# x read channel-major from the host's layout with 1/rms spread by two GpSimd transfers, y turned by DMA transposes, and latents first, in a hybrid attention layer

## The chip, the cores and the metric

The kernel runs on one core of one Trainium2 chip. The metric is device time in microseconds (us) of one execution, the median of several. TensorE (PE in the rows) has a weight-load side of its own (PEld); VectorE is DVE, ScalarE ACT, GpSimd POOL. SP only issues transfers here; SPq and ACTq are the streams of transfers that SP and ScalarE issue. The transfers of all of them run on the same 16 DMA engines of the core.

## The reference, cut to what matters

x is 2048 tokens by 1024 channels, float32. One layer:

```python
h = x + W_out( concat[ GQA(xn) * silu(g_A), MLA(xn) * silu(g_B) ] ), xn = RMSNorm(x)

y = xf * lax.rsqrt(jnp.mean(xf * xf, axis=-1, keepdims=True) + EPS) * g      # rms_norm
proj = xn @ w_in          # 2464 columns: q, k, v, gate of A; query latent, kv latent, rotary key, gate of B
c_q = rms_norm(b_cq), c_kv = rms_norm(b_ckv)                                 # the latents, 384 and 256 wide
qb = c_q @ w_uq ; kvb = c_kv @ w_ukv                                         # queries, keys and values of B
# per-head rms_norm and 2-D rotary on q and k, softmax attention over all 2048 tokens, 8 heads of A, 4 of B
y = concat[y_a * silu(a_g), y_b * silu(b_g)] ; h = x + y @ w_out
```

## The kernel before, in words

The work is in three phases that follow one another; phase 2 (attention) is not touched. Every large product is taken in three float16 matmuls: a float32 operand is split into a high part (its float16 rounding) and a low part (the rest), and high*high, high*low and low*high are summed. ScalarE makes high parts, VectorE low parts.

**Phase 1** (`phase1`) goes over 16 tiles of 128 tokens. TensorE contracts over partitions, so its left operand `xT` must have channels on partitions, and x arrives with tokens on them. For tile t: ScalarE squares and sums x (`x_hi`, L372), takes the root, VectorE the reciprocal (`x_rstd`, L494), ScalarE writes x * 1/rms as float16 (`xh`, L379), VectorE the rest (`x_lo`, `xl`, L502); TensorE turns both by 16 products with the identity (`transpose_x`, L659), and VectorE copies them out of PSUM (`xt_evac`, L508). The turn of tile t+1 lies inside tile t, between the products `ukv1` and `bg`. TensorE's order inside a tile is `cq, ckv, aq, akv`, the turn of the latents (`transpose_latents`, L671), `ag, uq, ukv0, ukv1`, the turn of x for the next tile, `bg` (all products L639); the last two tiles run a slightly other list (`LATE`), in which tile 14 has no `bg` of its own. Its results go through three PSUM banks (`ring`), which ScalarE empties (`evac`, L385). Head norms and rotary are a long chain on VectorE (L559 to L609), which begins when `ukv1` has been read out and squared (L461), and ends in the next tile; then `z_hi` and `z_lo` (L392, L514) split the finished rows, and two DMA transposes on SP's queue (`turn_z`, L307, L309) turn them, 13 blocks of 128x128 each. On both engines the steps of a tile stand in the order: x of the next tile and z of the one before, then the latents. In the first tile the weights are split as they arrive (`split_hi` L409, `split_lo` L522; pieces 0 to 7 are `cq, ckv, uq, ukv, aq, akv, ag, bg`), through raw buffers that SP refills when a piece has been split. A transfer on SP's queue waits in order: what stands behind a waiting one isn't issued.

**Phase 3** (`phase3`) again goes over 16 tiles: load the gate pre-activations G and attention outputs YA, YB (`load_yg`, L1220 to L1222), silu on ScalarE (L1257), gate on VectorE (L1295, L1296), split into `yh` (ScalarE, L1272) and `yl` (VectorE, L1323), turn both on TensorE (`turn`, L1342; that of tile t+1 lies between the two output halves of tile t), copy the turned tiles out of PSUM on ScalarE (`yT`, L1282), 48 matmuls of 512 columns (L1356), add the residual on VectorE (L1306), store (L1235). SP issues all loads and stores; its order in tile t is loads of t+2, then the wait for the residual of t, its store, and the load of x for t+2. On VectorE the gate of t+1 stands before the residual of t-1.

Of the kernel before, what the change touches and what calls it, by code (L numbers as in the profile page):

```python
# [24 lines left out]
P = 128  # L25
# [54 lines left out]
def phase1(nc, early, x, w_in, w_uq, w_ukv, g_in, g_cq, g_ckv, g_heads, trig, eye, QA, QBd, KBd, VA, VB, G):  # L80
    with ExitStack() as ctx:
# [17 lines left out]
        xin = sb("xin", [P, 2, D])  # L99
# [3 lines left out]
        xh = sb("xh", [P, D], F16)  # L103
        xl = sb("xl", [P, D], F16)
# [23 lines left out]
        xtp = [ps(f"xtp{i}", [P, KT, P], F16) for i in range(2)]  # L128
# [4 lines left out]
        s_x = [sem("x_loaded0"), sem("x_loaded1")]  # L133
# [7 lines left out]
        s_ax = sem("act_x_chain")  # L141
        s_dx = sem("dve_x")
        s_xtp = sem("xT_in_psum")
        s_xt = sem("xT_in_sbuf")
# [101 lines left out]
        def _(sp):  # L246
            sp.dma_start(xin[:, 0, :], xt[0]).then_inc(s_x[0], 16)
# [4 lines left out]
            for n in range(len(pieces)):  # L252
# [14 lines left out]
            def tile(i, h, first, last):  # L267
# [6 lines left out]
                if not last:  # L274

                    sp.wait_ge(s_dx, t * 2 + 2)
                    sp.dma_start(xin[:, h, :], xt[t + 2]).then_inc(s_x[h], 16)
# [75 lines left out]

        @block.gpsimd
        def _(pool):
            pool.memset(va[:, :, 2 * DA:2 * DA + 1], 1.0).then_inc(s_ones, 1)
# [8 lines left out]

        @block.scalar
        def _(act):
            def x_hi(t, h):

                st = stat[:, h, :]  # L370
                act.wait_ge(s_x[h], x_count(t, h))
                act.activation(junk[:, 0:D], xin[:, h, :], ACT.Square, accum_out=st[:, 0:1]).then_inc(s_ax, 1)  # L372
                act.wait_ge(s_ax, t * 3 + 1)
                act.activation(st[:, 1:2], st[:, 0:1], ACT.Sqrt, bias=eps[:, :], scale=1.0 / D).then_inc(s_ax, 1)
                act.wait_ge(s_dx, t * 2 + 1)
                if not zero(t):

                    act.wait_ge(s_xtp, t * 2)
                act.activation(xh[:, :], xin[:, h, :], ACT.Copy, scale=st[:, 2:3]).then_inc(s_ax, 1)  # L379
# [31 lines left out]
            def tile(i, h, first, last):  # L411
# [3 lines left out]
                if not (last and h == 1):  # L415
                    x_hi(t + 1, 1 - h)
# [990 lines left out]
```

## Time and profile before

| | |
|---|---|
| median of 3 runs | 1676.17 us (1674.85 to 1676.73) |
| the profiled execution's own time | 1674.67 us |
| its span, from first to last instruction | 1672.5 us |
| phase 1, until the first instruction of phase 2 | about 0 to 532 us |
| phase 2 | about 532 to 1463 us |
| phase 3 | about 1463 to 1672.5 us |
| TensorE busy over the span | 1566.9 us, 94% |
| VectorE, ScalarE, GpSimd | 71%, 65%, 34% |
| the 16 DMA engines | 38.2% |

Shares over the whole span mix three stages with different limits, so they say little about this change, which touches the first and the last. What counts is which wait ends last in each of these two, and that is read from the timeline of each engine and from the chain of waits. The profiled execution lies 1.5 us under the median.

### The profile page before, as it was taken

To read this page: it belongs to the slowest core of one execution; us is meant where nothing else is said; L and a number is where in the kernel's file an instruction comes from. 1 tells how busy PE (TensorE), PEld (TensorE's weight loads), DVE (VectorE), ACT (ScalarE), POOL (GpSimd) and SP (SyncE) were. 2 spreads that over 40 slices of the span, in tenths; PEclk is the share of its full clock that TensorE was granted. 3 is DMA by queue.
4 is the path that set the end of the run, shared out by engine and by line. 5 is a ranking of instruction groups with operands and counts; after the bars stand their busy time and mean duration, and the time that the engine had idled before them with its cause. 6 is when DMAs were issued, how large, how long until landed. Compare 5 with 4: busy or idle time off the path is not lost. (4 is left out here: it accounts for less than half of the span.)

```text
span 1672.5 us, 38256 instructions
## 1 busy us (share of the span) xinstructions
PE 1566.9 (94%) x13808; PEld 914.9 (55%) x13808; DVE 1181.3 (71%) x1664; ACT 1083.8 (65%) x1410; POOL 565.4 (34%) x478
## 2 busy tenths in 40 slices
PE   5899999999993799999999999999999999869998
PEld 2456555565551355665566556656665665534444
DVE  6665464654644889988998899889888988443322
ACT  8444444444431588888888888888888888643322
POOL 0100000000000356666666566656666665600000
PEclk9999999999996899999999999999999999979999
DMA  8343343353246422432243224322432243045563
GB/s 299 94 113 92 92 127 88 100 127 92 79 98 144 150 64 64 92 79 62 59 95 79 62 59 95 79 62 59 95 78 63 59 95 75 15 151 184 168 193 109
DMA packets 296351, 166.77 MB, mean 100 GB/s; under 512 B 118256, under 2 KB 279536, under 8 KB 296304
## 3 DMA queue, kind: packets, MB, share of 16 engines
q1 hardware_dynamic: 295824, 165.97, 38.2%
q8 instruction: 27, 0.44, 0.1%
q10 hardware_dynamic: 480, 0.20, 0.0%
q14 instruction: 20, 0.16, 0.0%
HBM read 109.85 MB, written 40.92 MB: 90 GB/s over the span
## 5 line engine op out<-in xcount | busy, mean ns | idle before, releaser
L940 POOL TENSOR_TENSOR p_pl<-p_p,p_ph 128x512 f16<-128x512 f32 x384 | 502.0, 1313 | 789.7 <-ACT p_ph L976 729.8
L991 DVE TENSOR_REDUCE p_part<-p_mx 128x2 f32<-128x1024 f32 x384 | 468.3, 1220 | 86.2 <-PE p_mx L1067 68.3
L967 ACT ACTIVATE p_p<-p_st 128x1024 f32<-128x1024 f32 x384 | 391.3, 1019 | 125.9 <-PE p_st L1099 68.1
L639 PE MATMUL p_ring<-p_w_hi,p_xT 128*128 128x512 f16 (+3 forms) x1536 | 389.2, 339 | 13.5 <-DVE p_w_lo L522 10.3
L976 ACT ACTIVATE p_ph<-p_p 128x1024 f16<-128x1024 f32 x336 | 355.3, 1057 | 18.3
L1019 DVE TENSOR_TENSOR p_pl<-p_p,p_ph 128x512 f16<-128x512 f32 x384 | 325.8, 849 | 10.3 <-ACT p_ph L976 9.4
L639 PE MATMUL p_ring<-p_w_lo,p_xT 128*128 128x512 f16 (+3 forms) x768 | 260.2, 339 | 0.0
L639 PEld LDWEIGHTS p_ring<-p_w_hi,p_xT 128*128 128x128 f16 x1536 | 151.1, 98 | 136.0 <-issue 12.9
L1131 PE MATMUL p_acc<-p_vas,p_ph 128*128 128x129 f16 x2048 | 207.9, 221 | 0.0
L1132 PE MATMUL p_acc<-p_vas,p_pl 128*128 128x65 f16 x2048 | 201.0, 193 | 0.0
L1131 PEld LDWEIGHTS p_acc<-p_vas,p_ph 128*128 128x128 f16 x2048 | 180.6, 97 | 36.4 <-issue 14.3
L1098 PE MATMUL p_st<-early 128*128 128x512 f16 x512 | 194.7, 380 | 0.0
L1099 PE MATMUL p_st<-early 128*128 128x512 f16 x512 | 194.6, 380 | 0.0
L1132 PEld LDWEIGHTS p_acc<-p_vas,p_pl 128*128 128x128 f16 x2048 | 181.4, 98 | 13.5
L1135 PE MATMUL p_acc<-p_vbs,p_ph 128*128 128x129 f16 x1024 | 185.9, 221 | 0.0
L1137 PE MATMUL p_acc<-p_vbs,p_pl 128*128 128x129 f16 x1024 | 184.6, 222 | 0.0
L1136 PE MATMUL p_acc<-p_vbs,p_ph 128*128 128x128 f16 x1024 | 184.2, 219 | 0.0
L1356 PE MATMUL p_po<-p_w_hi,p_yT 128*128 128x512 f16 x512 | 158.8, 383 | 8.7 <-ACT p_yT L1282 4.3
L1067 PE MATMUL p_mx<-early 64*128 64x512 f16 x512 | 104.4, 404 | 45.7 <-DVE p_kb L1041 24.5
L1135 PEld LDWEIGHTS p_acc<-p_vbs,p_ph 128*128 128x128 f16 x1024 | 100.9, 99 | 50.4 <-issue 39.9
L639 PEld LDWEIGHTS p_ring<-p_w_lo,p_xT 128*128 128x128 f16 x768 | 75.5, 98 | 53.6 <-issue 0.5
L508 DVE COPY p_xT<-p_xtp 128x1024 f16<-128x1024 f16 x32 | 20.7, 686 | 117.8 <-PE p_xtp L659 117.8
(130 smaller groups left out, 2027.4 us busy)
## 6 DMA issues: line engine op xcount, KB each, us to landing
p_vbs<-scratch_vb SPq DMA_DIRECT2D x16, 1028.0 KB, 6.1
p_xin<-in_x SPq DMA_DIRECT2D x16, 512.0 KB, 3.8
scratch_g<-p_g SPq DMA_DIRECT2D x16, 512.0 KB, 2.6
p_kb<-scratch_kb SPq DMA_DIRECT2D x32, 256.0 KB, 5.3
p_gt<-scratch_g SPq DMA_DIRECT2D x16, 512.0 KB, 4.7
p_xr<-in_x SPq DMA_DIRECT2D x16, 512.0 KB, 4.1
out<-p_res SPq DMA_DIRECT2D x16, 512.0 KB, 3.0
early<-in_w_in SPq DMA_DIRECT2D x6, 1024.0 KB, 7.0
```

Source lines behind the costliest of these rows:

```text
L639: last = pe.matmul(ring_t[:, 0:w], a, b, start=(k == 0 and m == 0), stop=(k == len(steps) - 1 and m == len(terms) - 1))
L940: pool.tensor_tensor(pl[:, s % NP, 1, :], p32[:, s % N32, QB:], ph[:, s % NP, 1, :], ALU.subtract).then_inc(s_lop, 1)
L967: act.activation(p32[:, s % N32, :], st[:, s % 2, :, :].rearrange("p a b -> p (a b)"), ACT.Exp, scale=scale).then_inc(s_exp, 1)
L976: act.activation(ph[:, s % NP, :, :].rearrange("p a b -> p (a b)"), p32[:, s % N32, :], ACT.Copy).then_inc(s_hi, 1)
L991: dve.tensor_reduce(part[:, e // MPAIRS % 3, 2 * c:2 * c + 2], mx[:, :, :], AX, ALU.max).then_inc(s_red, 1)
L1019: dve.tensor_tensor(pl[:, s % NP, 0, :], p32[:, s % N32, 0:QB], ph[:, s % NP, 0, :], ALU.subtract).then_inc(s_lo, 1)
L1098: pe.matmul(out, ka_hl[g][:, keys], qa_hh[g][:, :], start=True, stop=False)
L1099: end = pe.matmul(out, ka_up[g][:, keys], qa_ml[g][:, :], start=False, stop=True)
L1131: pe.matmul(a, hi, vas[:, t, g, :], start=new, stop=False, skip_group_check=True)
L1132: last = pe.matmul(a[:, DA:], lo, vas[:, t, g, DA:], start=False, stop=end, skip_group_check=True)
L1135: pe.matmul(a, hi, vbs[:, t, DVB:], start=new, stop=False, skip_group_check=True)
L1137: last = pe.matmul(a, lo, vbs[:, t, DVB:], start=False, stop=end, skip_group_check=True)
```

## The change

In phase 1, x is read a second time, channel-major (`x_cols`, laid out by the host: for each tile a 128-partition block of 8 x 128 tokens). The token-major copy (`xin`, now one buffer) serves only for the sum of squares. The 128 values 1/rms of a tile stand one per partition; two transfers issued by GpSimd write them to DRAM (`RS`) and read them back as a row copied to all partitions (`rsb`). VectorE multiplies `xcol` by it in place (`x_scale`), ScalarE writes the high part straight into `xT`, VectorE the low part. TensorE's turn of x, the PSUM tiles `xtp` and `xt_evac` are gone. The statistics of a tile are taken two tiles ahead. In a tile, both engines now do the latents before z and x. In the first tile, the statistics of tiles 0 and 1 and the whole of x for tile 0 stand between `split(0)` and `split(1)`.

In phase 3, `yh` and `yl` get two buffers each and are turned by two DMA transposes on SP's queue (8 blocks each); TensorE's turn, the PSUM tiles `tp` and ScalarE's copies are gone. From tile 2 on, ScalarE issues `load_yg`, after the silu of the next tile; SP keeps the transposes, the store and the x load.

```diff
@@ phase 1, SP
+                if n == 0:
+                    sp.dma_start(xcol[:, :, :], x_cols[0]).then_inc(s_xc, 16)
                 if n == 1:
-                    sp.dma_start(xin[:, 1, :], xt[1]).then_inc(s_x[1], 16)
+                    load_x(1)               # waits s_ax >= 2
+                if n == 3:
+                    load_x(2)               # waits s_ax >= 4
+                if n == 4:
+                    sp.wait_ge(s_xt, 1)
+                    sp.dma_start(xcol[:, :, :], x_cols[1]).then_inc(s_xc, 16)
@@ phase 1, GpSimd
+        def spread_rstd(eng, t):
+            eng.wait_ge(s_dx, t + 1)
+            eng.dma_start(RS[t], stat[:, t % 2, 2:3]).then_inc(s_rs, 16)
+            eng.wait_ge(s_rs, t * 16 + 16)
+            if t > 1:
+                eng.wait_ge(s_xs, t - 1)
+            eng.dma_start(rsb[:, t % 2, :], RS[t].partition_broadcast(P)).then_inc(s_rsb[t % 2], 16)
@@ phase 1, VectorE
+            def x_scale(t, h):
+                dve.wait_ge(s_xc, t * 16 + 16)
+                dve.wait_ge(s_rsb[h], (t - h) * 8 + 16)
+                dve.tensor_tensor(xcol[:, :, :], xcol[:, :, :], rsb[:, h, :].unsqueeze(1).to_broadcast([P, KT, P]),
+                                  ALU.mult).then_inc(s_xs, 1)
             def x_lo(t, h):
+                dve.wait_ge(s_xh, t + 1)
+                dve.tensor_tensor(xT[:, h, 1], xcol[:, :, :], xT[:, h, 0], ALU.subtract).then_inc(s_xt, 1)
@@ phase 1, VectorE, before the loop
             x_rstd(0, 0)
-            x_lo(0, 0)
-            xt_evac(0, 0)
-            dve.wait_ge(s_const, 64)
-            for n in range(5):
+            dve.wait_ge(s_const, 64)
+            split_lo(0)
+            x_rstd(1, 1)
+            x_scale(0, 0)
+            x_lo(0, 0)
+            for n in range(1, 5):
                 split_lo(n)
@@ phase 1, TensorE
-                if not (last and h == 1):
-                    transpose_x(t + 1, 1 - h)
@@ phase 3, SP
+            def turn(t, h, free):
+                sp.wait_ge(s_yh, t + 1)
+                if free:
+                    sp.wait_ge(s_po, t * 2 - 2)
+                sp.dma_start_transpose(yT[:, h, 0], yh[:, h, :]).then_inc(s_yt[h], 16)
+                sp.wait_ge(s_yl, t + 1)
+                sp.dma_start_transpose(yT[:, h, 1], yl[:, h, :]).then_inc(s_ytl[h], 16)
             def tile(t, h, i, first, last):
-                if not last:
-                    sp.wait_ge(s_yg, t * 2 + 2)
-                    load_yg(t + 2, h)
+                if not (last and h == 1):
+                    turn(t + 1, 1 - h, not (first and h == 0))
                 sp.wait_ge(s_res, t * 2 + 2)
                 sp.dma_start(ot[t], res[:, h, :]).then_inc(s_out[h], 16)
@@ phase 3, ScalarE, tile t
-                for s in range(2):
-                    act.wait_ge(s_tp, t * 2 + s + 1)
-                    if not first:
-                        act.wait_ge(s_po, t * 2 - 2)
-                    act.activation(yT[:, h, s], tp[s][:, :, :], ACT.Copy).then_inc(s_yt, 1)
+                if not last:
+                    load_yg(act, t + 2, h)
@@ phase 3, TensorE, tile t
-                    if c == 0 and not (last and h == 1):
-                        turn(t + 1, False)
```

The first place is ScalarE in tile 1 of phase 1, from the gate's read-out (`p1_g`) on. Before:

```order
L372 ACTIVATE p1_junk,p1_stat<-p1_xin 128x1024
L374 ACTIVATE p1_stat<-p1_stat,p1_eps 128x1
L379 ACTIVATE p1_xh<-p1_xin,p1_stat 128x1024
L392 ACTIVATE p1_zh<-p1_R 128x640
L393 ACTIVATE p1_zh<-p1_R 128x8x96
L385 ACTIVATE p1_cq32<-p1_ring0 128x384
L385 ACTIVATE p1_ckv32<-p1_ring1 128x288
L426 ACTIVATE p1_junk,p1_lstat<-p1_cq32 128x384
```

and with the change:

```order
L403 ACTIVATE p1_junk,p1_stat<-p1_xin 128x1024
L407 ACTIVATE p1_stat<-p1_stat,p1_eps 128x1
L421 ACTIVATE p1_cq32<-p1_ring0 128x384
L421 ACTIVATE p1_ckv32<-p1_ring1 128x288
L460 ACTIVATE p1_junk,p1_lstat<-p1_cq32 128x384
L461 ACTIVATE p1_junk,p1_lstat<-p1_ckv32 128x256
L463 ACTIVATE p1_lstat<-p1_lstat,p1_eps 128x1
L464 ACTIVATE p1_lstat<-p1_lstat,p1_eps 128x1
L470 ACTIVATE p1_lat_hi<-p1_cq32,p1_lstat 128x384
L471 ACTIVATE p1_lat_hi<-p1_ckv32,p1_lstat 128x256
L428 ACTIVATE p1_zh<-p1_R 128x640
L415 ACTIVATE p1_xT<-p1_xcol 128x1024
```

The second list leaves out the second half of `zh` (L429), which stands between its last two rows. The read-outs of `cq` and `ckv` and the latents' high parts moved ahead of z and x.

The second place is the start of phase 1 on VectorE. Before:

```order
L494 RECIPROCAL p_stat<-p_stat 128x1
L502 SCALAR_TENSOR_TENSOR p_xl<-p_xin,p_stat,p_xh 128x1024
L508 COPY p_xT<-p_xtp 128x1024 x2
L522 SCALAR_TENSOR_TENSOR p_w_lo<-early,p_gin,p_w_hi 128x384 x8
L522 SCALAR_TENSOR_TENSOR p_w_lo<-early,p_gin,p_w_hi 128x288 x8
```

and with the change:

```order
L535 RECIPROCAL p_stat<-p_stat 128x1
L560 SCALAR_TENSOR_TENSOR p_w_lo<-early,p_gin,p_w_hi 128x384 x8
L535 RECIPROCAL p_stat<-p_stat 128x1
L541 TENSOR_TENSOR p_xcol<-p_xcol,p_rsb 128x1024
L546 TENSOR_TENSOR p_xT<-p_xcol,p_xT 128x1024
L560 SCALAR_TENSOR_TENSOR p_w_lo<-early,p_gin,p_w_hi 128x288 x8
```

The low parts of the first weight piece moved ahead of x, and tile 1's reciprocal (the second L535) stands before tile 0's x.

The third place is SP in a tile of phase 3. Before:

```order
L1220 DMA p3_ya<-scratch_ya 128x4x64 x2
L1221 DMA p3_yb<-scratch_yb 128x4x128
L1222 DMA p3_gt<-scratch_g 128x1024
L1235 DMA out_0<-p3_res 128x1024
L1237 DMA p3_xr<-in_x 128x1024
```

and with the change:

```order
L1251 DMA_TRANSPOSE p3_yT<-p3_yh 128x8x128
L1253 DMA_TRANSPOSE p3_yT<-p3_yl 128x8x128
L1263 DMA out_0<-p3_res 128x1024
L1265 DMA p3_xr<-in_x 128x1024
```

The four loads left SP for ScalarE, and two transposes took their place.

## Rows read from the trace of the kernel before

**Rows 1.** Windows: us, busy PE, PEld, DVE, ACT, POOL; clock, DMA share, GB/s

```profile
200.00:470.00 270.00, 270.00 (x1726) 158.65 (x1725) 148.57 (x288) 121.78 (x288) 0.00 (x0) 1.00 0.40 99
1500.00:1624.00 124.00, 120.08 (x671) 57.66 (x669) 39.51 (x54) 41.69 (x44) 0.00 (x0) 1.00 0.56 175
```

**Rows 2.** Timeline of PE, a middle tile of phase 1: start, us, what

```profile
255.11 0.33 PE L671 MATMUL p_trp<-p_ident,p_lat_hi 128*128 128x128 f16 x3
...
264.25 0.61 PE L659 MATMUL p_xtp<-p_ident,p_xh 128*128 128x128 f16 x8
...
265.15 0.38 PE L639 MATMUL p_ring<-p_w_hi,p_xT 128*128 128x512 f16 x1
```

**Rows 3.** Timeline of DVE, end of the rotary chain, same tile

```profile
246.04 1.16 DVE L609 TENSOR_TENSOR p_R<-p_R,p_T 128x640 f32<-128x640 f32 x2
```

**Rows 4.** Timeline of PE, tile 1; in brackets the idle time before

```profile
57.25 0.34 PE L639 MATMUL p_ring<-p_w_hi,p_xT 128*128 128x384 f16 x1 [0.30 <-DVE p_xT L508]
...
70.99 0.28 PE L639 MATMUL p_ring<-p_w_hi,p_xT 128*128 128x256 f16 x1 [1.54 <-ACT p_cq L385]
...
75.83 0.33 PE L671 MATMUL p_trp<-p_ident,p_lat_hi 128*128 128x128 f16 x3 [2.05 <-issue]
```

**Rows 5.** Timeline of PE, from the turn for tile 15 to its latents

```profile
473.39 0.61 PE L659 MATMUL p_xtp<-p_ident,p_xh 128*128 128x128 f16 x8
...
492.35 0.33 PE L671 MATMUL p_trp<-p_ident,p_lat_hi 128*128 128x128 f16 x3 [1.48 <-issue]
```

**Rows 6.** Timeline of DVE over the same stretch

```profile
484.98 1.16 DVE L609 TENSOR_TENSOR p_R<-p_R,p_T 128x640 f32<-128x640 f32 x2
...
489.91 0.17 DVE L537 RECIPROCAL p_lstat<-p_lstat 128x2 f32<-128x2 f32 x1 [0.54 <-ACT p_lstat L430]
```

**Rows 7.** Timelines of ACT and of DVE in the first tile

```profile
8.14 0.29 ACT L374 ACTIVATE p_stat<-p_stat,p_eps 128x1 f32<-128x1 f32 x1
9.72 7.55 ACT L409 ACTIVATE p_w_hi<-early,p_gin 128x384 f16<-128x384 f32 x16
...
27.71 1.04 ACT L372 ACTIVATE p_junk<-p_xin 128x1024 f32<-128x1024 f32 x1
...
39.63 5.38 DVE L522 SCALAR_TENSOR_TENSOR p_w_lo<-early,p_gin,p_w_hi 128x512 f16<-128x512 f32 x8
...
67.86 0.15 DVE L494 RECIPROCAL p_stat<-p_stat 128x1 f32<-128x1 f32 x1
```

**Rows 8.** DMA, 5 to 17 us: queue (packets, MB, share); issue (KB, us to landing)

```profile
q1 hardware_dynamic: 2914, 4.59, 103.8%
p_xin<-in_x SPq DMA_DIRECT2D x1, 512.0 KB, 8.6
```

**Rows 9.** DMA issues of the first 75 us

```profile
p_gains<-in_g_heads SPq DMA_DIRECT2D x1, 704.0 KB, 9.6
...
scratch_va<-p_va SPq DMA_DIRECT2D x1, 64.5 KB, 1.6
```

**Rows 10.** The chain that ended last, one tile of phase 3, and its end

```profile
1506.58 0.36 SPq L1235
...
1509.71 4.72 DMA p_gt<-scratch_g
...
1516.24 0.69 DVE p_yg L1296
...
1653.18 15.55 PE p_po L1356 x72
```

**Rows 11.** Chain, the start of phase 3's products

```profile
1480.65 7.47 PE p_po L1356 x24
```

**Rows 12.** DMA, 515 to 522 us, where hardly anything but two turns of z runs

```profile
q1 hardware_dynamic: 3392, 0.85, 65.0%
...
p_zT<-p_zl SPq DMA_TRANSPOSE x1, 4.2
```

**Rows 13.** Groups of phase 3: count, then busy us, mean ns

```profile
L1323 DVE TENSOR_TENSOR p_yl<-p_yg,p_yh 128x1024 f16<-128x1024 f32 x16 | 19.6, 1225 | 6.8 <-ACT p_yh L1272 6.8
```

More of the change, by code:

```diff
@@ L98, in phase1 @@
         eps = sb("eps", [P, 1])
-        xin = sb("xin", [P, 2, D])
+        xin = sb("xin", [P, D])
+        xcol = sb("xcol", [P, KT, P])
+        rsb = sb("rsb", [P, 2, P])
         trg = sb("trg", [P, 2, 192])
@@ L437, in tile @@
                 act.activation(lat_hi[:, RQ:], ckv32[:, 0:RKV], ACT.Copy, scale=ls[:, 5:6]).then_inc(s_lat, 1)
+                if not (first and h == 0):
+                    z_hi(t - 1, 1 - h)
+                if not (last and h == 1):
+                    x_hi(t + 1, 1 - h)
                 evac(t, "aq", slice(0, 512), (Rh[:, 0:512], whole))
@@ L527, in tile @@
                 Rh = R[:, h, :]
+                if not last:
+                    x_rstd(t + 2, h)
                 if not (last and h == 1):
-                    x_rstd(t + 1, 1 - h)
-                if not (first and h == 0):
-                    z_lo(t - 1, 1 - h)
-                if not (last and h == 1):
-                    x_lo(t + 1, 1 - h)
+                    x_scale(t + 1, 1 - h)
                 ls = lstat[:, h, :]
@@ L545, in tile @@
                                          op0=ALU.mult, op1=ALU.subtract).then_inc(s_dlat, 1)
+                if not (first and h == 0):
+                    z_lo(t - 1, 1 - h)
+                if not (last and h == 1):
+                    x_lo(t + 1, 1 - h)
                 dve.wait_ge(s_ltp, t * 2 + 1)
@@ L552, in tile @@
                         split_lo(n)
-                if not (last and h == 1):
-                    xt_evac(t + 1, 1 - h)
                 dve.wait_ge(s_sq, t + 1)
@@ L1237, in tile @@
                     sp.dma_start(xr[:, h, :], xt[t + 2]).then_inc(s_x[h], 16)
-            loop(sp, tile)
+            for t in range(TILES):
+                tile(t, t % 2, t // 2, t < 2, t >= TILES - 2)
             for h in range(2):
                 sp.wait_ge(s_out[h], PAIRS * 16)
-        @block.gpsimd
-        def _(pool):
-            pool.memset(eye[:, :], 0.0).then_inc(s_eye, 1)
-            pool.wait_ge(s_eye, 1)
-            pool.affine_select(out=eye[:, :], in_=eye[:, :], compare_op=ALU.not_equal, fill=1.0,
-                               base=0, pattern=[[-1, P]], channel_multiplier=1).then_inc(s_eye, 1)
         @block.scalar
@@ L1335, in _ @@
         def _(pe):
-            def turn(t, first):
-                for s, src in enumerate((yh, yl)):
-                    pe.wait_ge(s_yh if s == 0 else s_yl, t + 1)
-                    if not first:
-                        pe.wait_ge(s_yt, t * 2 - 1 + s)
-                    for k in range(KT):
-                        last = pe.transpose(tp[s][:, k, :], src[:, k * P:(k + 1) * P], eye[:, :])
-                    last.then_inc(s_tp, 1)
             def tile(t, h, i, first, last):
-                pe.wait_ge(s_yt, t * 2 + 2)
+                pe.wait_ge(s_yt[h], i * 16 + 16)
+                pe.wait_ge(s_ytl[h], i * 16 + 16)
                 for c in range(2):
```

144 lines of the change are left out of this document (67 added, 77 removed).

## The prediction

> **What bounds the kernel now.** I read the windows first, then PE's timeline in each of the two phases that are touched, then, where PE waits, the timeline of the engine that it waits for. In the middle of phase 1 PE has work for all 270 us of 270, at the full granted clock [rows 1], while VectorE is busy 148.6 and ScalarE 121.8: what leaves PE's stream there shortens the phase one for one, as long as nothing else takes more than its place. At the two ends of phase 1 PE does wait: in tile 1 for 1.54 and 2.05 us [rows 4], in tile 15, which has no `bg` products ahead of it, for the turned x and for the latents [rows 5]. Phase 3 is different. Its 16 tiles run from 1480.65 to 1668.73 (1653.18 + 15.55), 11.76 us each [rows 10, 11], but 24 products take 5.18 us (15.55/3), so a tile's 48 take 10.37 and the turn 0.9. The chain does not run over PE there; each tile it runs SP's store, its loads, the 4.72 us of the load of G, silu, gate, residual and again the store [rows 10]: SP loads G of tile t+2 only after it has stored tile t-1, and the residual of t stands behind the gate that needs it. So phase 3 is a loop of latencies a little longer than PE's own work; PE is busy 120.1 of 124 us [rows 1].
>
> **Phase 1, middle.** The turn of x holds PE from 264.25 to 265.15 [rows 2], 0.90 us per tile. Its place is taken by nothing on PE. What could grow into the gap: VectorE loses the scaled subtraction and two copies and gets two passes over 1024 columns, priced by the nearest row, 1.22 us each [rows 13]; ScalarE's count of passes is the same. The latents: the rotary chain ends at 247.20 [rows 3]; then come a reciprocal, `x_scale` (1.25), and from the latents' reciprocal to PE's turn of them 2.44 (489.91 to 492.35, [rows 5, 6]), together 251.1, where PE asks at 255.1 - 0.9 = 254.2 [rows 2]. 3 us of cover. The two GpSimd transfers of a tile have a whole tile, 29 us, between `x_rstd` and `x_scale`; the slowest landing in these rows is 9.6 us and the quickest 1.6 [rows 9], so a pair is 3 to 19 us and hidden either way. The load of `xcol` waits for `x_lo` of the tile before, and the turn of z stands behind it on SP; that delays z by some 4 us, and z has until the next tile. From tile 1's latents to tile 14's there are 13 turns: **-11.7 us**.
>
> **Phase 1, tile 15.** The rotary chain ends at 486.14 [rows 6]; today z and x come first. With latents first the turn of the latents may start at 486.14 + 2.44 = 488.6. PE's own path: `cq` can begin at 473.39, where the turn of x stood [rows 5], and the products up to the latents take 15.0 us (57.25 to 75.83 less 1.54 and 2.05, [rows 4]): 488.4. So 488.6 in place of 492.35: **-3.75 us**, the last turn in it. From there to the end of phase 1 (the rotary chain, z's split, its turn, the stores) the order is unchanged and moves as one.
>
> **Phase 1, start.** Here the change costs first and recovers later. `xin` has one buffer, so its second load waits for the first statistics, which end at 8.43 [rows 7] (before it was issued with the weights, and landed 8.6 us later, about 14.3, [rows 8]); the 16 DMA engines are full then, 4.59 MB in 12 us [rows 8], and `xcol` adds 0.5 MB, 1.35 us. So x of tile 1 lands at 15.7, its statistics end at 17.3, `x_scale(0)` runs 17.5 to 18.75, ScalarE's high part 19.9, the low part 21.2; PE starts near 21.3. ScalarE's weight pieces 1 to 4 wait for all that: they run now from the middle of row 9.72 (13.5) to 27.71 [rows 7], 12.0 us without their 2.2 us of waits, and will end at 31.9, 4.2 later. The stretch from there to `split_lo` of piece 6 on VectorE, 39.63 today [rows 7], loses `xh` and its wait (1.5) and gains the net of `x_lo(1)` (0.6): it comes 3.4 us late, and the rest of tile 0 with it. `xt_evac` no longer stands before tile 1 (0.3), nor the 1.54 and 2.05 us in tile 1, since the `cq` read-out and latents no longer queue behind z. PE's path: `bg` ends at 56.95 + 3.4 = 60.3, plus 15.0 is 75.3. VectorE's path: its chain ends at 67.86 today [rows 7], plus 3.4 less the 1.2 of `xt_evac`, 70.1; plus 0.15, 1.25 and 2.44, 73.9. PE's governs: 75.3 against 75.83, **-0.5 us**. What is unknown is the pair of transfers for tile 0, for which 8.6 to 17.5 us is free: at the slow end, 2 x 9.6, they are 10.3 us late, and all of it comes through (+10). At the quick end nothing is gained, since the statistics of tile 1 bind. I take 4 us a leg (64 KB or less while the engines are full, nearer to the 1.6 us row by size, to the 9.6 by load): hidden. GpSimd's pair for tile 2 stands behind its memsets, which end some 3.4 us later than today, near 64.5, and is wanted by 70: 5.5 us, near the edge too, worth 0 to +3.
>
> The Trainium skill ("DMA: Bandwidth & Descriptors", section "Anatomy of one DMA") puts one at about 2.0 us fixed plus the bytes; no run here shows one yet. By it a pair is 4 to 5 us and both places are covered.
>
> **Phase 3, start.** G is now loaded first (it was issued 1.5 us after the first load), so silu follows ScalarE's split and table load and not G, 1.3 us earlier; then `yh` is ready near 1472.2 and `yl` at 1473.5. Today PE's turn, behind ScalarE's second split and silu, lets the products start at 1480.65 [rows 11]. A transpose of 13 blocks lands 4.2 us after its issue [rows 12]; one of 8 takes no longer: the start is 1477.6, **-3.0 us**. It could be 1.2 us sooner or, behind the other start-up loads, 3 later.
>
> **Phase 3, tiles.** Today 188.1 us from first to last product. The first 24 take 7.47, 2.29 over 5.18, after PE had mostly stood idle, and will again. With loads issued by ScalarE a whole tile earlier, the loop over SP is open: G of t+2 no longer waits for a store. What is left is PE, 16 x 10.37 + 2.3 = 168.2, **-19.9 us**, if the turned y is there. That is a new wait and I follow it. From the end E of PE's tile t: residual 0.85; SP's store and load of x 0.8; then the two transposes for t+2, which have to land before PE has done t+1, at E + 10.37. `yl` is ready at E + 2.1. Store and x are 1 MB ahead of them on the queue, 3.3 us at the load's rate. The engines' time: two turns of z, 26 blocks, fill 65% of 7 us, 4.55 us [rows 12], so 16 blocks are 2.8. Landing at E + 1.7 + 3.3 + 2.8 + 1, about 8.8: cover of 1.6 us. ScalarE's loads (four issues near 0.4 us) come in the same tile at about E + 5.5 to 7.5. All DMA together: 0.56 of 11.76 is 6.6 us [rows 1], and 2.8 is 9.4 of 10.37. So the DMA engines go to nine tenths, and this is the weakest term.
>
> The Trainium skill ("Advanced Engine Details and Errata", X-Bar Transpose) says that transposing transfers run at 350 to 400 GB/s. The row shows 0.85 MB in 4.55 us, 187 GB/s; by the page the 16 blocks would be 1.4 us and the cover 3 us.
>
> **Sum.** -0.5 - 11.7 - 3.75 - 3.0 - 19.9 = -38.9 on the profiled execution's 1674.67: 1635.8. The median of the runs shown is 1.5 above that execution, its lowest run 0.2: I add 0.9, **1636.7 us**.
>
> **The rivals.**
> - *The DMA engines become the bound of phase 3.* If the transposes take as long as landing to landing in the row for z (about 6 us for 26 blocks, 3.7 for 16) and the engines idle as much between pieces as they do today (0.6 us a tile), a tile is 6.6 + 3.7 + 0.6 = 10.9 us; or a landing at E + 12 makes it (12 + 10.37)/2 = 11.2, since a late pair is felt every second tile. 16 x 0.55 to 0.85 gives +9 to +14: 1646 to 1651. For it speaks nine tenths of load, against it that today's loads come in one burst and are then idle. The Trainium skill ("DMA: Bandwidth & Descriptors", "Issuing engines are not separate DMA queues") says that issuing from a second engine saves only issue time; that agrees with pricing the moved loads at nothing in bandwidth, and the gain claimed is the wait removed.
> - *The start is late.* The GpSimd pair for tile 0 lands at 27.8: +10, 1647.
> - *Phase 3 gives back everything and more.* The transposes land so late that a tile is (L + 10.37)/2 with L over 15.6 us, above which the 38.9 are gone ((15.6 + 10.37)/2 is 13.0; 15 x 2.6 = 39). At L = 20, as when each transpose waits for every queued transfer of both engines, it is 1709. Against it: 4.2 us in the row, next to other traffic.
> - *More than the sum.* Transposes at the page's rate and a quick start: 1631.
>
> **Chances.** Forecast (1630 to 1643) 0.58; DMA bound 0.20; late start, alone or with it, 0.13; more than the sum 0.04; slower 0.04; about unchanged 0.01. 0.2% (3.4 us) is about what a measurement of this kernel can tell from no change. Faster 0.95, within it 0.01, slower 0.04. The range of 8 in 10 goes from 1629 to 1652, into the two cases above the forecast.
>
> **What the new profile would show.** Middle of phase 1: a tile of 28.97 us, no PE idle. Tile 1's latents near 75.3, PE's first product near 21. Tile 15's latents 3.8 us earlier against phase 1's course. Phase 3: 10.4 us a tile, the chain on PE's products and not on the load of G, PE waiting for `yT` nowhere after the start. I am wrong if PE's idle time before phase 3's products is put down to a DMA, if DMA share in phase 3 stays at 0.9 with longer tiles, or if `x_scale(0)` starts behind `rsb`.

## The result, and the profile after

1654.34 us median (1653.71 to 1655.98) against 1676.45 for the kernel before in the same comparison: the ratio is 0.9871, 95% interval 0.9854 to 0.9888, or -21.6 us (18.8 to 24.5). The forecast was -38.9 and 1636.7 us, with a range up to 1652, so the time lies 2.3 us above the range. The direction was right; a little over half of the forecast's sum came. The profiled execution took 1655.98 us, the slowest of the four; its span is 1654.1 against 1672.5. The parts read from it below therefore add up to 18.4 us, and 20.5 us of the forecast are missing in them.

The page of the changed kernel (busy time and share; then tenths in 40 slices, the granted clock, the DMA share and GB/s):

```profile
PE 1536.6 (93%) x13296; PEld 887.7 (54%) x13296; DVE 1179.5 (71%) x1648; ACT 1054.3 (64%) x1378; POOL 582.6 (35%) x508
...
PEclk9999999999997799999999999999999999979999
DMA  9555545644446532423232233223322432179894
GB/s 244 182 103 138 124 118 129 142 130 113 120 89 144 166 65 61 95 64 74 64 81 64 74 78 80 63 67 89 79 63 60 96 79 63 40 185 250 231 235 122
```

PE's busy time fell by 30.3 us, its share by one point: the work was taken away, and a part of the gap stayed open. Where, two points in time tell. Phase 2's first instruction is issued at 528.67 us (before 532.03), phase 3's first at 1459.32 (before 1463.25); so phase 1 and what it hands on gave some 3.9 us of the 15.95 forecast. From phase 3's first load to its last residual it took 191.0 us (before 205.5): 14.5 of the 22.9 forecast.

**Phase 1.** PE's timeline: the first product, the latents of tile 1, those of tile 15 (start, us, what, idle time before):

```profile
29.46 0.48 PE L677 MATMUL p_ring<-p_w_hi,p_xT 128*128 128x384 f16 x1 [29.46 <-ACT p_w_hi L445]
...
86.35 0.33 PE L697 MATMUL p_trp<-p_ident,p_lat_hi 128*128 128x128 f16 x3 [2.57 <-issue]
...
488.89 0.33 PE L697 MATMUL p_trp<-p_ident,p_lat_hi 128*128 128x128 f16 x3 [0.29 <-issue]
```

The latents of tile 1 stand at 86.35, not at the 75.3 forecast and the 75.83 of [rows 4]: 10.5 us lost. From there to tile 15's it is 402.54 us against 416.52 [rows 4, 5]: 14.0 won of the 15.45 forecast. So the loss lies in the first 86 us. GpSimd's timeline there:

```profile
9.09 0.71 POOL L374 DMA_DIRECT2D scratch_rs<-p_stat  x1 [8.63 <-DVE p_stat L535]
19.30 0.55 POOL L378 DMA_DIRECT2D p_rsb<-scratch_rs  x1 [9.50 <-DMA scratch_rs<-p_stat]
...
71.20 0.55 POOL L374 DMA_DIRECT2D scratch_rs<-p_stat  x1
78.72 0.54 POOL L378 DMA_DIRECT2D p_rsb<-scratch_rs  x1 [6.98 <-DMA scratch_rs<-p_stat]
```

and what waits for it, VectorE (first row, and again in tile 1) and ScalarE:

```profile
25.78 1.22 DVE L541 TENSOR_TENSOR p_xcol<-p_xcol,p_rsb 128x1024 f32<-128x1024 f32 x1 [4.27 <-DMA p_rsb<-scratch_rs]
...
82.77 1.22 DVE L541 TENSOR_TENSOR p_xcol<-p_xcol,p_rsb 128x1024 f32<-128x1024 f32 x1 [4.16 <-DMA p_rsb<-scratch_rs]
...
19.84 1.06 ACT L403 ACTIVATE p_junk<-p_xin 128x1024 f32<-128x1024 f32 x1 [7.21 <-DMA p_xin<-in_x]
27.04 1.06 ACT L415 ACTIVATE p_xT<-p_xcol 128x1024 f16<-128x1024 f32 x1 [5.73 <-DVE p_xcol L541]
```

The write of 128 values, 0.5 KB, takes 10.2 us until the read behind it is issued, the read back 6.5: the pair is 16.7 us where the forecast took 8. But ScalarE's 7.21 us are not a wait for the pair: they are for `xin` of tile 1, a transfer on SP's queue. The DMA view of 14 to 24 us (40 slices of 0.25 us) says why:

```profile
DMA  9993444599922892493992336963156999999701
GB/s 386 449 268 123 154 164 178 191 236 201 148 86 109 166 123 86 162 139 143 145 143 111 141 123 129 141 86 68 37 172 258 406 393 426 320 258 111 45 0 49
```

The rate falls from about 390 GB/s to mostly 86 to 200 at 14.6 us, and comes back near 21.7. The write of 1/rms was issued at 9.09 and landed by 19.3: the rate falls 5.5 us behind its issue, and stays low some 2 us behind its landing. The engines are not at rest: their busy share from 14 to 21 us is 1.08 in the mean, and between 0.47 and 2.39 from one us to the next.

**Phase 3.** The chain of waits over some tiles (start, us, what):

```profile
1499.95 9.29 PE p_po L1366 x43
...
1509.27 0.70 DVE p_res L1324
...
1509.99 0.35 SPq L1263
...
1510.38 0.43 SPq L1265
...
1510.91 1.70 SPq L1251
...
1512.66 8.95 DMA p_yT<-p_yl
...
1521.84 10.54 PE p_po L1366 x48
1532.39 0.02 issue
...
1535.82 6.99 DMA p_yT<-p_yl
1542.81 0.24 issue
1543.05 10.55 PE p_po L1366 x48
...
1598.30 51.98 PE p_po L1366 x240
```

It runs over PE, but also over the new transfer. PE ends a tile at 1509.25; the turned `yl` for the tile after the next lands at 1521.61, E + 12.4, where the forecast had E + 8.8. In the next piece it is 1532.39 to 1542.81, E + 10.4. From 1521.84 to 1598.30 there are 7 tiles, 10.92 us each. The windows of before are in [rows 1]; after:

```profile
1480.00:1600.00 120.00, 114.47 (x526) 50.82 (x525) 40.12 (x54) 21.17 (x22) 0.00 (x0) 1.00 0.95 237
```

### The profile page after: what moved, and what is told of

It reads as the page before. It is cut to its first block and busy times, and to the rows that moved or that the text cites. A ratio compares the mean times of both kernels' runs of the same rounds, so it can differ in the third digit from the quotient of the medians.

```text
span 1654.1 us, 37099 instructions
## 1 busy us (share of the span) xinstructions
PE 1536.6 (93%) x13296; PEld 887.7 (54%) x13296; DVE 1179.5 (71%) x1648; ACT 1054.3 (64%) x1378; POOL 582.6 (35%) x508
## 5 line engine op out<-in xcount | busy, mean ns | idle before, releaser
L998 ACT ACTIVATE p_ph<-p_p 128x1024 f16<-128x1024 f32 x336 | 355.2, 1057 | 18.4
L1041 DVE TENSOR_TENSOR p_pl<-p_p,p_ph 128x512 f16<-128x512 f32 x384 | 325.5, 848 | 10.2 <-ACT p_ph L998 9.4
L1153 PEld LDWEIGHTS p_acc<-p_vas,p_ph 128*128 128x128 f16 x2048 | 180.6, 97 | 36.5 <-issue 14.5
L1366 PE MATMUL p_po<-p_w_hi,p_yT 128*128 128x512 f16 x512 | 154.8, 382 | 27.1 <-DMA p_yT<-p_yl 26.2
L595 DVE TENSOR_REDUCE p_rstat<-p_sq 128x10 f32<-128x640 f32 x16 | 13.1, 820 | 147.0 <-ACT p_sq L499 147.0
L1324 DVE SCALAR_TENSOR_TENSOR p_res<-p_po,p_xr 128x512 f32<-128x512 f32 x32 | 22.1, 692 | 118.5 <-PE p_po L1366 118.5
```

The lines of the kernel that those rows point to most:

```text
L998: act.activation(ph[:, s % NP, :, :].rearrange("p a b -> p (a b)"), p32[:, s % N32, :], ACT.Copy).then_inc(s_hi, 1)
L1041: dve.tensor_tensor(pl[:, s % NP, 0, :], p32[:, s % N32, 0:QB], ph[:, s % NP, 0, :], ALU.subtract).then_inc(s_lo, 1)
L1153: pe.matmul(a, hi, vas[:, t, g, :], start=new, stop=False, skip_group_check=True)
L1366: mm = pe.matmul(po[h][c][:, :], yT[:, h, s, k, :], w[:, k, cols], start=(k == 0 and m == 0), stop=(k == KT - 1 and m == 2))
```

## The experiments

The ratio of each run is to the kernel before on the same chip.

**1. The halves apart.** `e1_phase3_only` is phase 1 of before with the new phase 3, `e2_phase1_only` the reverse.

> Phase 1 of before with phase 3 of the changed kernel. Theory (the loss against the forecast lies in both phases, and the phases add): phase 3 takes 191.0 us from its first load to its last residual, as in the changed kernel, where before took 205.5, so the kernel is 14.5 us faster than before, about 1662. Rival (phase 3's gain hangs on how phase 1 leaves things, for instance where x and the scratch tensors lie): the gain differs from 14.5 by more than 2.

> Phase 1 of the changed kernel with phase 3 of before. Theory: phase 2 begins 3.9 us earlier than before and phase 3 costs 205.5 again, so about 4 us faster than before, 1672.5. Rival, as for the run on phase 3 alone: the two gains do not add up to 18 to 22 us.

Measured: phase 3 alone 1659.89 us, ratio 0.9903 (0.9887 to 0.9920), -16.3; phase 1 alone 1673.71 us, ratio 0.9982 (0.9973 to 0.9992), -3.0. The sum, -19.3, agrees with the change's -21.6 within the intervals. Phase 3 took 190.3 us in the first of them. So no disturbance of one half by the other is seen, and each fell short by itself. In the profiled execution of the second, the slowest of its ten, phase 2 begins at 532.23, no earlier than in the kernel before; its start of phase 1 was 3 us later than the change's, with the same code (more on this at the end of the next section).

**2. The order of the first tile.**

```diff
             x_stat(0, 0)
             split_hi(0)
+            split_hi(1)
             x_stat(1, 1)
+            split_hi(2)
+            split_hi(3)
             x_hi(0, 0)
-            for n in range(1, 5):
-                split_hi(n)
+            split_hi(4)
```

and the same on VectorE: weights are split while x is waited for.

> The changed kernel, with the splits of weight pieces 1 to 3 ahead of x of tile 0 on ScalarE and VectorE, which stand idle 7.2 and 5.7 us there. Theory (the start is lost because every weight split waits behind a round trip through DRAM of 17 us): the round trip is as long, PE's first product no earlier than 28, but piece 4 is split from 28 to 33.5 instead of 34.6 to 39.6, and the latents of tile 1 are turned 6 us earlier, so 6 us faster than the changed kernel, about 1648.5. Rival (PE's late first product, 29.5 against 13.7, is what costs): no change, 1654.

Measured: 1657.11 us, ratio 0.9884 (0.9868 to 0.9901). A miss: about 2 us behind the change, not 6 ahead of it. ScalarE's timeline:

```profile
20.44 1.81 ACT L445 ACTIVATE p_w_hi<-early,p_gin 128x288 f16<-128x288 f32 x4 [5.60 <-DMA early<-in_w_in]
...
34.94 1.33 ACT L445 ACTIVATE p_w_hi<-early,p_gin 128x512 f16<-128x512 f32 x2 [4.78 <-DMA early<-in_w_in]
```

The engine that was to use the idle time now waits for weights. An order of work doesn't help when all transfers are late; that turned the theory from "x waits for the pair" to "everything waits for DMA", which the next experiments test.

**3. The pair for tile 2 ahead of GpSimd's fills.**

```diff
+            spread_rstd(pool, 2)
             pool.wait_ge(s_whi, rows_before[-1])
             pool.wait_ge(s_wlo, rows_before[-1])
             for g in range(GA):
                 pool.memset(early.ka_up[g][0:64, :], ONE)
                 pool.memset(early.qa_ml[g][0:64, :], 0.0)
-            for t in range(2, TILES):
+            for t in range(3, TILES):
```

> The changed kernel, with GpSimd's pair of transfers for tile 2 ahead of its four memsets, which wait for the last weight piece. Theory: the pair lands before 60 instead of at 82.7, the 4.2 us wait of VectorE before the second scaling of x in the loop goes and PE's wait of 2.6 us before the latents of tile 1 with it; PE's clock does not dip after it: 2.6 to 4 us faster than the changed kernel, about 1651. Rival (PE's wait comes from ScalarE or from the rotary chain): the same, 1654.

Measured: 1652.96 us, ratio 0.9865 (0.9849 to 0.9882), not told apart from the change by the medians. In its profile the pair for tile 2 is issued at 41.5 and 52.9, PE no longer waits ahead of tile 1's latents (84.41 us, 1.9 earlier), and tile 15's stand at 485.28, 3.6 earlier. So the wait is there and goes with its cause; that the kernel gains as much as the profile shows is not shown by the medians.

**4. The small write alone.** `e5_small_write_only` is the kernel before, plus

```diff
+            def store_rstd(t):
+                pool.wait_ge(s_dx, t * 2 + 1)
+                ...
+                pool.dma_start(RS[t], stat[:, t % 2, 2:3]).then_inc(s_rs[t % 2], 16)
```

> The kernel before, with one thing of the change alone: GpSimd writes each tile's 1/rms (128 values of 4 bytes, one from each partition) to DRAM as soon as it is there, and nobody reads it. Theory A (the small write itself slows all DMA beside it): the write takes about 10 us from issue to landing, and from 9 to 20 us the page's row of GB/s falls from some 390 to between 100 and 200 while the DMA engines stay busy, as in the changed kernel. PE's first product, 13.7 us before, does not wait for it, but the weights land late, and tile 1's latents come 3 to 8 us after the 75.83 of before: 1679 to 1684 us. Theory B (the fall has another cause, as the second load of x behind the first statistics): GB/s stays near 390 and the time is that of before within 0.2%. Either way the middle of phase 1 is unchanged, since nothing waits there.

`e12_apart` is the same with each of the 128 values 512 bytes from the next: `RS` is 16 x 128 x 128, and the write goes to `RS[t][:, 0:1]`.

> The kernel before with the same unread write of 1/rms by GpSimd as in the run that took that write alone, 128 pieces of 4 bytes at the same moments, but each piece 512 bytes from the next in DRAM. If the slow landing and the fall of the rate come from 128 pieces that meet in the same 512 bytes, the write lands in 2 to 3 us also at the start, GB/s stays near 390 from 9 to 20 us, and the time is that of before within 0.1%. If they come from pieces of 4 bytes (the forms run had pieces of 8 bytes apart), the write takes 9 to 10 us here too, GB/s falls to between 120 and 200, and the time is 2 to 4 us over before.

Measured: 1678.71 us, ratio 1.0020 (1.0010 to 1.0029) for the first, 1676.55 us, ratio 1.0003 (0.9994 to 1.0012) for the second. The first one's GB/s from 14 to 24 us (slices of 0.25 us):

```profile
GB/s 399 301 123 135 123 135 160 154 240 234 178 123 141 135 147 123 129 123 135 197 209 184 190 168 197 164 156 209 279 328 344 418 385 385 401 401 410 401 410 434
```

The same of the second, whose queue has next to nothing to move from 17.2 to 19 us, as in the kernel before:

```profile
GB/s 399 393 387 406 418 387 369 418 406 393 418 332 135 12 0 0 0 57 74 57 164 295 319 401 401 401 451 393 385 369 352 393 393 410 401 418 410 401 418 401
```

One write of 0.5 KB that nobody reads takes the rate of all transfers beside it to less than half, for some 6.5 us from 14.5 on (it is issued at 8.96 and lands in 10.0). Its second write, issued at 31.97 and landed in 10.1 us, does it again: the rate is 37 to 130 GB/s from 39 to 43.5 us, where the second run has 259 to 421. The same 128 pieces of 4 bytes, 512 bytes apart, land in 5.1 us (each of the two writes of the first 30 us), slower than the 2 to 3 us expected, and cost the others nothing that can be seen. Theory A holds in the first, and the second names the property: pieces of 4 bytes that lie side by side. (The spread `RS` is 128 times as large, so the tensors behind it lie elsewhere in DRAM; no run moved them alone.) The time lost was 3.4 us, at the low end of what was expected: the kernel before has its first x turned at 11.3, before the rate falls, and only its weights come late; its latents of tile 1 stand at 78.0 in place of 75.8.

**5. Who issues it.** `e6_write_by_act` moves the write to ScalarE:

```diff
-            eng.dma_start(RS[t], stat[:, t % 2, 2:3]).then_inc(s_rs, 16)
+                act.dma_start(RS[t], stat[:, h, 2:3]).then_inc(s_rs[h], 16)
```

> The changed kernel, but the write of 1/rms is issued by ScalarE instead of GpSimd; the read back stays with GpSimd. If the 10 us and the fall of the rate belong to GpSimd's queue, the write lands in 2 to 3 us, the rate stays near 390 GB/s, the first product comes near 22 in place of 29.5 us, and the time is 5 to 8 us below the changed kernel's 1654.3: 1646 to 1649. If they belong to the form of the transfer (128 pieces of 4 bytes behind full DMA engines), the write takes 8 to 10 us here too and the time stays within 1651 to 1657.

Measured: 1651.95 us, ratio 0.9857 (0.9841 to 0.9873). The first write lands in 10.8 us from this queue too (9.9 in the change), the rate from 14 to 21 us is 147 GB/s, PE's first product comes at 28.98. The transfer is slow, not GpSimd. By the ratios this kernel is 2.3 us ahead of the change, which the overlapping intervals do not tell from nothing. Its profile fits the wait of experiment 3: this write no longer stands behind GpSimd's fills, and PE comes to tile 1's latents at 85.99 without a wait.

**6. Forms of small writes**, one after another, by GpSimd, beside the kernel before.

```diff
+                dst, src = [(RS[0][n], pad[:, 0:1]), (RS[1][n][:, 0:2], pad[:, 0:2]), (RS[2][n], pad[:, 0:16]),
+                            (RS[3][n], pad[:, :]), (RS[4][n], pad[0:4, :])][form]
```

> The kernel before, and beside its work GpSimd writes small pieces to DRAM that nobody reads, each form behind the landing of the one before it: at the start, while the weights load, 128 pieces of 8 bytes that lie 512 bytes apart in DRAM, then 4 pieces of 128 bytes, 128 of 64 bytes, 128 of 128 bytes; in tiles 3, 6 and 9 all of these and the change's own form, 128 pieces of 4 bytes side by side. Theory A (the price is that of 128 pieces under some size, whatever lies beside them): the pieces of 8 bytes apart cost about 10 us too, 4 pieces of 128 bytes some 2 us, and 64 and 128 bytes a piece are cheaper than 4. Theory B (the price comes from 128 engines' writes into the same 512 bytes of DRAM): the form side by side takes 9 to 10 us and the form apart 2 to 4 us. The time of the whole kernel is expected within 1676 to 1690 us and tells nothing apart.

DMA issues of the whole run (KB each, median us to landing): `close` is 128 pieces of 4 bytes side by side, `apart` 128 of 8 bytes 512 bytes apart, `four` 4 of 128 bytes, `line` and `row` 128 of 64 and of 128 bytes, side by side. One of the four of each (none of `close`) ran at the start, while the weights load; the others in tiles 3, 6 and 9:

```profile
scratch_apart<-p_pad POOLq DMA_DIRECT2D x4, 1.0 KB, 2.1
scratch_four<-p_pad POOLq DMA_DIRECT2D x4, 0.5 KB, 2.2
scratch_line<-p_pad POOLq DMA_DIRECT2D x4, 8.0 KB, 1.7
scratch_row<-p_pad POOLq DMA_DIRECT2D x4, 16.0 KB, 1.7
scratch_close<-p_pad POOLq DMA_DIRECT2D x3, 0.5 KB, 8.8
```

1677.75 us, ratio 1.0006 (0.9995 to 1.0016). Theory B: 0.5 KB as 4 pieces takes 2.2 us, as 128 pieces side by side 8.8, and 32 times as many bytes from 128 partitions 1.7. Lying side by side is not enough by itself: `line` and `row` do so too, with 8 and 4 pieces in every 512 bytes, and are quick. At the start, under load, `apart`, `four`, `line` and `row` took 3.8, 5.0, 4.7 and 2.6 us.

**7. Phase 1 without the pair.** `e7_ones_product` drops `xin`, `RS` and both transfers; the sum of squares comes from `xcol`, and the sum over partitions from one product with ones. With that it also loads 0.5 MB less a tile, takes the statistics one tile ahead instead of two, and moves a few steps: `xcol` of tile 0 is loaded first, weight piece 1 is split ahead of tile 0's high part, and `x_hi` stands behind the read-out of `aq`.

```diff
+                pool.tensor_tensor(xs1[:, :], xsq[:, 0:128], xsq[:, 128:256], ALU.add).then_inc(s_xp, 1)
...
+                pe.matmul(xss[:, :], ones[:, :], xs1[:, :], start=True, stop=True).then_inc(s_ss, 1)
...
+                act.activation(root[:, :], xss[:, :], ACT.Sqrt, bias=eps[:, :], scale=1.0 / D).then_inc(s_ax, 1)
...
+                dve.reciprocal(rsb[:, :], root[:, :]).then_inc(s_dx, 1)
```

> The changed kernel without the two GpSimd transfers and without x in rows: ScalarE squares the channel-major x, GpSimd adds its eight blocks to one of 128x128, TensorE multiplies that by a tile of ones, so that the sum of squares stands in every partition, and ScalarE and VectorE make 1/rms of it there (the partial sums are rounded to float16). My theory (the start of phase 1 lost its time to the pair of transfers for tiles 0 and 2 and to the fallen rate beside them): tile 1's latents come near 72 to 74 us in place of 86.35, the rate stays near 390 GB/s in the first 20 us, and the time is 12 to 14 us less, 1640 to 1643; a tile in the middle pays up to 0.1 us for the product of ones. Rival (the weights' arrival and ScalarE's queue set the start, whatever brings 1/rms): tile 1's latents stay above 82 us and the time above 1650.

Measured: 1641.57 us, ratio 0.9803 (0.9780 to 0.9825), 11.4 us below the change by the ratios. PE's timeline (the same three places), and the window of 14 to 21 us (busy us by engine, clock, share, GB/s):

```profile
20.73 0.48 PE L674 MATMUL p_ring<-p_w_hi,p_xT 128*128 128x384 f16 x1 [10.69 <-DVE p_xT L544]
...
74.66 0.33 PE L694 MATMUL p_trp<-p_ident,p_lat_hi 128*128 128x128 f16 x3 [0.87 <-issue]
...
476.24 0.33 PE L694 MATMUL p_trp<-p_ident,p_lat_hi 128*128 128x128 f16 x3 [0.28 <-issue]
```

```profile
14.00:21.00 7.00, 0.27 (x1) 0.14 (x2) 6.96 (x12) 7.00 (x14) 0.00 (x0) 1.00 1.04 389
```

The first product at 20.7, the latents of tile 1 at 74.7, 401.58 us to tile 15, phase 2's first instruction at 516.06, 15.97 us before that of the kernel before: the forecast had 21.3 and 75.3, -15.45 for the stretch to tile 15 (here -14.94) and -15.95. The rate stays at 389. No run puts the pieces 512 bytes apart in the change itself, so how much of the 11.4 us that alone would bring is open.

**8. Phase 3, a third buffer.** `e8_three_buffers`: the turn of tile t+2 is issued before the store of t, and `yl` made a tile ahead.

```diff
-        yT = sb("yT", [P, 2, 2, KT, P], F16)
+        yT = sb("yT", [P, 3, 2, KT, P], F16)
@@ SP, tile t, ahead of the store
-                if not (last and h == 1):
-                    turn(t + 1, 1 - h, not (first and h == 0))
+                if t == 0:
+                    turn(1)
+                if not last:
+                    turn(t + 2)
@@ VectorE, tile t, ahead of the residual of t-1
+                    y_lo(t + 1)
```

> The changed kernel with three buffers for the turned y in phase 3 in place of two: VectorE makes yl of tile t+1 right after its gate, and SyncE issues the turn of tile t+2 before the store of tile t, not behind it. The same bytes move. If the late landing of the transposes (a latency behind the end of a tile's products) makes the 10.92 us of a tile, the tile falls to 10.4 to 10.6 and the time by 5 to 8 us, to 1646 to 1649. If the DMA engines' throughput makes it (10.4 us of engine time per tile, at a share of 0.95), the tile stays at 10.7 to 10.9 us and the time at 1651 to 1655, with the DMA share at 0.96 or more.

Measured: 1650.60 us, ratio 0.9844 (0.9828 to 0.9861), -4.5 against the change by the ratios, whose intervals just overlap; phase 3 itself took 185.2 us (191.0). The chain, and the window:

```profile
1478.16 167.83 PE p_po L1371 x768
```

```profile
1480.00:1600.00 120.00, 120.00 (x553) 54.16 (x551) 44.88 (x59) 24.04 (x24) 0.00 (x0) 0.99 1.04 256
```

All 768 products in one piece of 167.83 us, where the forecast had 168.2; 10.49 us a tile. The transposes land no sooner (7.8 and 7.4 us after their issue, medians from 1500 to 1598; after the change 4.9 and 7.3). A late landing no longer matters, and the same bytes go at 256 GB/s instead of 237. So throughput wasn't the limit; a DMA share of 0.95 did not mean that the engines had no more to give. The run also writes out the loop over the tiles of phase 3. That this is not what helped is read from the change, whose last 5 tiles run over the loop's seam in one piece of 51.98 us, 10.40 a tile.

**9. One order alone.** `e10_yl_first` takes only VectorE's part of that edit, its loop written out too, with two buffers.

```diff
+            y_lo(0)
             def tile(t, h, i, first, last):
-                dve.wait_ge(s_yh, t + 1)
-                ...
-                dve.tensor_tensor(yl[:, h, :], yg[:, h, :], yh[:, h, :], ALU.subtract).then_inc(s_yl, 1)
                 ...
                 if not (last and h == 1):
                     gate(t + 1, 1 - h, i if h == 0 else i + 1, first and h == 0)
+                    y_lo(t + 1)
```

> The changed kernel with one order turned on VectorE in phase 3: yl of tile t+1 is made before the residual of tile t-1 and not behind it; two buffers of turned y stay, and all else. If the late yl is what lets the second transpose land late, the tile falls from 10.92 to 10.5 to 10.7 us and the time by 3 to 6 us (1648 to 1651). If the free buffer (a turn starts only when PE has left it) is what binds, the time stays within 2 us of the changed kernel's 1654.3 and the tile at 10.8 to 10.9 us.

Measured: 1670.51 us (1660.56 to 1677.10), ratio 0.9962 (0.9937 to 0.9987). Both expectations missed: 15 us slower than the change, and with a wide spread. In the profiled execution phase 3 takes 203.9 us (191.0 in the change), and it begins 5.4 us later (1464.69), behind phases whose code is the change's. The chain:

```profile
1519.41 10.77 DMA p_yT<-p_yl
1530.18 0.24 issue
1530.42 11.89 PE p_po L1373 x48
...
1545.79 11.98 DMA p_yT<-p_yl
1557.77 0.24 issue
```

Without `yl` between the residual and the gate, ScalarE's loads of the next tile come a pass of VectorE sooner. In the tile from 1526 to 1543 they are issued from 1528.7 on, and the transpose of `yl` at 1529.8, 1.1 us behind them; in the change it is 1535.81 and 1535.82, side by side. In this run the transposes land 9.0 and 9.1 us after their issue (medians), in the chain above 14.2 and 15.5 us behind the end of PE's tile (1516.0 and 1542.3), and PE's next products then run below the full clock (0.93 from 1480 to 1600). That the loads ahead of the transpose are the cause is read from these timelines; no run moved the loads alone. What is shown: with two buffers this order makes phase 3 12.9 us longer, with three (experiment 8, the same order on VectorE) PE waits nowhere.

**10. Both mends together**, `e11_both` (7 and 8 in one).

> The sum of squares by a product with ones (the change's pair of small transfers gone) and three buffers of turned y in phase 3, together. The two gains lie in different phases, so they should add: the start of phase 1 as in the first of the two (tile 1's latents near 74.7 us, phase 2 at 516), and a tile of phase 3 at 10.49 us. 1641.6 less 4 to 6 us: 1635 to 1638, which is the time that the prediction gave for the change. If the start of phase 3 takes the gain back (the first products came 1.5 us later behind the first load with three buffers), 1638 to 1640.

Measured: 1636.84 us (1636.66 to 1637.11), ratio 0.9764 (0.9748 to 0.9780), 17 to 18 us below the change. PE comes to tile 1's latents at 74.95. Phase 2's first instruction is issued at 515.86 us; 720 of the 768 products run in one piece:

```profile
1475.49 155.57 PE p_po L1381 x720
```

## Why the prediction was right and wrong

- **What bounds the kernel, and "Phase 1, middle": right.** -13.98 from tile 1's latents to tile 15's against -15.45 for this part and tile 15 together; in experiment 7, -14.94, and in experiment 3, where PE does not wait for tile 1's latents, -15.65. So the us and a half that the change lacks is the clock: it is 0.94 in the windows 50 to 80 and 80 to 110 us, and the products behind the wait at 86.35 run at the lower of the two levels, 1.2 GHz (0.63 us a row where 0.38 is usual).
- **"Phase 1, tile 15": right.** Latents at 488.89 with a wait of 0.29 us; they hang on PE's own path and VectorE's chain alike, as forecast.
- **"Phase 1, start": wrong, and this is the largest error, 10.5 to 11 us.** The step that failed is "I take 4 us a leg". The legs measured 10.2 and 6.5, so `x_scale(0)` started at 25.78 and not at 17.5, and PE at 29.46 and not at 21.3. The rows gave bounds of 3 to 19 us, and I chose by a row with the right size and the wrong form: the 64.5 KB of [rows 9] have some 500 bytes a partition, the write has 4. The rival "the start is late" priced the slow end at +10 and had 0.13. It named the place and the price, not the mechanism: the pair doesn't only land late, its write slows every transfer beside it (experiments 4 and 5), which is why `xin(1)` came at 19.8 in place of 15.7 and why an order that put weights first (experiment 2) lost. The step "GpSimd's pair for tile 2 ... worth 0 to +3" held: the pair came 2.57 us late for PE. The rest of the start fits: with the pair gone, experiment 7 gives 20.7 and 74.7 for the forecast's 21.3 and 75.3, though that run dropped the load of `xin` and moved steps as well, so it does not prove each term.
- The page "DMA: Bandwidth & Descriptors" of the Trainium skill, section "Anatomy of one DMA", has about 2.0 us for a small transfer. Four of the five forms agree in the median (1.7 to 2.2 us), but not under load at the start (2.6 to 5.0), and the one that the change uses took 6.4 to 10.8 in the change. By its rule a pair would be 4 to 5 us, an estimate, and this case (16.7) would have been priced further off than by the rows' upper end of 19.
- **"Phase 3, start": half right.** `yh` and `yl` were issued 9.1 and 10.4 us behind the first load, forecast 8.95 and 10.25. The step "one of 8 takes no longer" failed: issued at 1469.73, `yl` landed 6.3 us later, not 4.2. Start 1476.13, 16.8 us behind the first load, in place of 14.35: +2.5.
- **"Phase 3, tiles": wrong by 6 us.** PE's part was right (167.83 in experiment 8). The mis-sized term is "landing at E + 1.7 + 3.3 + 2.8 + 1, about 8.8": up to 1.7 it is exact (1510.87), then the landing took 10.7 and 8.7 us in place of 7.1, E + 12.4 and E + 10.4. The cover of 1.6 us was smaller than that error, and PE waits in every second or third tile. The transposes' engine time also was under-sized: 0.95 of 10.92 us is 10.4 a tile, less the 6.6 of before is 3.8, not 2.8 (an estimate: a share is no fixed cost, for in experiment 8 the same bytes give 1.04 of 10.49, 10.9 a tile). The Trainium skill's 350 to 400 GB/s for such transfers ("Advanced Engine Details and Errata", X-Bar Transpose) would make it 1.4; 16 blocks in 3.8 us are 138 GB/s, so the trace differs from it by more than from my estimate.
- **The rival "the DMA engines become the bound of phase 3"** gave 10.9 us a tile and got the number (10.92) for the wrong reason in its first form (throughput) and nearly the right one in its second (a late landing, felt every second tile). Experiment 8 parts them: same bytes, PE idle nowhere.
- **Both rivals came at once.** Each alone gave a time inside the range, 1646 to 1651 and 1647. All three signs of being wrong that the prediction named are there: `x_scale(0)` starts behind `rsb`, the DMA share of phase 3 is 0.95 with tiles of 10.92 us, and PE's 21.6 us ahead of phase 3's products are put down to the transpose of `yl`.
- **"Gives back everything and more"** did not happen in the change, but experiment 9 shows how near it is: with landings at E + 14.2 and E + 15.5 in the two tiles shown, phase 3 took 203.9 us, 1.6 less than before.

The size of the two waits is shown by the kernels without them: 11.4 us in experiment 7, with what else it changed, 4.5 in experiment 8, and with both 1636.84 us, where the forecast was 1636.7. That these two agree to 0.2 us is in part luck: in that run phase 3 took 185.3 us for a forecast of 182.6, since its first product comes 16.3 us behind the first load and not 14.35, and phase 2, which nothing touched, 1.3 us less than before. Two things stay open: by what mechanism pieces of 4 bytes that share a stretch of DRAM hold up everything else, and why the start of phase 1 differs by some us between profiled executions of the same phase 1 (tile 1's latents at 86.35 in the change, 86.81 in experiment 8, 89.60 in `e2_phase1_only`, 91.80 in experiment 9, behind a wait of 2.6 to 5.2 us).

## What to carry to other kernels

A transfer is priced by its form, and a nearest row is near only if the bytes per piece, and the way that they lie in DRAM, are alike; if a form is not in the trace, keep the whole range in the range. Before moving 128 values from partitions into a row by a write to DRAM, sum or spread them on an engine: with a product with ones, one instruction a tile on PE and three additions on GpSimd, the kernel was 11 us faster. If they must go to DRAM, lay them 512 bytes apart, as the second run of experiment 4 did; no run tried that in the change. Where a transfer takes an engine's place in a ring of two buffers, give it a third and issue it a tile ahead before asking whether the DMA engines are full.

## What the hardware showed that was not expected

- A write of 128 pieces of 4 bytes that lie side by side in DRAM (512 bytes in all) takes 6.4 to 10.8 us from issue to landing in the change (median 9.4), and about as long when ScalarE issues it; the same pieces 512 bytes apart took 1.8 to 5.1 us (median 3.6), the longest under full load. Pieces of 64 and 128 bytes side by side took 1.7.
- From 5.5 us behind the first one's issue to 2 us behind its landing, all transfers together drop from about 390 GB/s to mostly 120 to 200, with a DMA share of 1.05. How a write of 0.5 KB does that is not settled; that it takes pieces of 4 bytes side by side is what the two runs of experiment 4 show.
- A DMA share of 0.95 at 237 GB/s rose to 1.04 at 256 GB/s when the transfers were only issued earlier.
- A transpose of 8 blocks landed in 4.9 to 9.1 us (medians of the two transposes in the change and in experiments 8 and 9), kernels that differ in what is issued beside it and when.
